# An expert layer in two forms: 96 tokens gather the rows of their picked experts, 160 stay dense in plain float32

## The reference

```python
# 8 heads, 128 x 128 = 16384 single-neuron experts, top 16 per head: 128 picks a token
s1 = einsum('thd,kd->thk', q[:, :, 0], sub_k1);  v1, i1 = top_k(s1, 16)
s2 = einsum('thd,kd->thk', q[:, :, 1], sub_k2);  v2, i2 = top_k(s2, 16)
cand = (v1[..., :, None] + v2[..., None, :]).reshape(T, 8, 256)
vals, ci = top_k(cand, 16)
idx = i1[ci // 16] * 128 + i2[ci % 16];  gates = softmax(vals)
# for a token t with its 128 picks k:
h = einsum('tkd,td->tk', expert_u[idx], x)
a = gelu(h) * gates
out = einsum('tk,tkd->td', a, expert_v[idx])
```

## Time and profile before

| | us |
|---|---|
| median of 3 runs (1588.82 to 1589.45) | 1589.16 |
| span of the profiled execution | 1587.9 |
| the expert layer in it, 249.8 to 1023.7 | 773.9 |
| TensorE busy | 1556.2 |
| VectorE busy | 1253.3 |
| ScalarE busy | 806.6 |
| GpSimd busy | 105.1 |

### The profile page before, as it was taken

One profiled execution on the slowest core, in us unless ns is written; L12 is line 12 of the kernel. 1 busy time (PEld: TensorE's weight loads), 2 busy tenths in 40 slices (PEclk: granted clock), 3 DMA queues, 4 the chain that ended last, 5 costly groups with the idle time before them and its releaser, 6 DMA issues.

```text
span 1587.9 us, 26239 instructions
## 1 busy us (share of the span) xinstructions
PE 1556.2 (98%) x9128; PEld 1364.8 (86%) x9128; DVE 1253.3 (79%) x2167; ACT 806.6 (51%) x1231; POOL 105.1 (7%) x67
## 2 busy tenths in 40 slices
PE   8999899999999999999999999999999999999998
PEld 7888799999999888888888888888887988778886
DVE  5575669989999777777777777887878988688777
ACT  5545545457776333444444444554445757554444
POOL 0000177700000000000000000000000000000000
PEclk9999999999999999999999999999999999999999
DMA  5544444533334555555555555555554433445552
GB/s 219 192 153 176 158 149 168 180 142 110 106 109 182 190 202 189 187 183 186 188 193 193 192 185 185 198 197 187 190 185 147 162 130 107 159 166 192 185 185 106
DMA packets 39389, 270.47 MB, mean 170 GB/s; under 512 B 4881, under 2 KB 5393, under 8 KB 7074
## 3 DMA queue, kind: packets, MB, share of 16 engines
q1 hardware_dynamic: 37440, 266.45, 47.3%
q10 hardware_dynamic: 1890, 3.24, 0.6%
HBM read 268.62 MB, written 1.05 MB: 170 GB/s over the span
## 4 chain that ended last, share of the span: by engine, by line
PE 80%; DVE 14%; issue 3%; ACT 2%; DVEq 1%; DMA 0%; SPq 0%; ACTq 0%
PE ps L737 52%; PE ps L770 17%; PE ps L772 7%; DVE wlo L567 2%; DVE wlo L2171 2%; DVE raw L2142 2%; PE ps L769 1%; DVE XT L1899 1%; DVE wlo L2142 1%; DVE whi L2142 1%; DVE arena L2519 0%; PE ps L1013 0%; PE ps L1202 0%; PE ps L980 0%; DVE raw L2155 0%
## 5 line engine op out<-in xcount | busy, mean ns | idle before, releaser
L770 PE MATMUL ps<-XT,whi 128*128 128x512 f32 x1200 | 429.2, 398 | 2.9 <-DVE XT L1899 1.9
L737 PE MATMUL ps<-XT,whi 128*128 128x256 f32 x1696 | 311.0, 285 | 1.6 <-DVE wlo L567 0.9
L772 PE MATMUL ps<-XT,wlo 128*128 128x256 f32 x1050 | 294.5, 281 | 0.0
L550 ACT ACTIVATE whi<-raw 128x1024 fp32r<-128x1024 f32 x194 | 204.3, 1059 | 171.8 <-PE ps L737 130.5
L737 PE MATMUL ps<-whi,HAh 128*128 128x512 f32 x696 | 272.2, 391 | 1.0 <-DVE wlo L567 0.8
L737 PE MATMUL ps<-wlo,HAh 128*128 128x512 f32 x696 | 271.2, 390 | 0.0
L737 PE MATMUL ps<-whi,HAl 128*128 128x512 f32 x696 | 270.8, 389 | 0.0
L567 DVE TENSOR_TENSOR wlo<-raw,whi 128x1024 fp32r<-128x1024 f32 x174 | 211.1, 1221 | 71.3 <-ACT whi L550 69.6
L737 PEld LDWEIGHTS ps<-XT,whi 128*128 128x128 f32 x1696 | 263.6, 192 | 2.3 <-DVE wlo L567 1.3
L770 PEld LDWEIGHTS ps<-XT,whi 128*128 128x128 f32 x1200 | 222.4, 188 | 49.4 <-issue 2.3
L737 PE MATMUL ps<-XT,wlo 128*128 128x256 f32 x848 | 239.8, 283 | 0.0
(11 more groups left out here) (292 smaller groups left out, 1919.9 us busy)
## 6 DMA issues: line engine op xcount, KB each, us to landing
raw<-in_experts SPq DMA_DIRECT2D x128, 1024.0 KB, 4.7
raw<-in_panels SPq DMA_DIRECT2D x58, 1024.0 KB, 4.8
raw<-in_ffa SPq DMA_DIRECT2D x33, 1024.0 KB, 4.8
raw<-in_ffb SPq DMA_DIRECT2D x33, 1024.0 KB, 4.7
arena<-in_row_post ACTq DMA_DIRECT2D x3, 512.0 KB, 4.5
X<-in_x SPq DMA_DIRECT2D x2, 512.0 KB, 5.6
arena<-in_row_ln ACTq DMA_DIRECT2D x2, 256.0 KB, 4.1
arena<-in_row_post SPq DMA_DIRECT2D x1, 512.0 KB, 5.7
```

The costliest lines, as they stand in the source:

```text
L550: act.activation(whi[:, buf(p), :], half(item_of(p), p % 2), ACT.Copy).then_inc(part_hi, 1)
L737: last = pe.matmul(out, x if w_moving else w, w if w_moving else x, start=start and n == 0, stop=stop and n == 2)
L770: last = pe.matmul(out, wh[:, k], XT[:, k], start=k == 0, stop=k == NK - 1)
L772: pe.matmul(out[:, T:], wl[:, k], XTh[:, k], start=False, stop=False)
```

## The change

The 256 tokens are divided. Tokens 0 to 95 (SPARSE, on partitions 0 to 95 of tile 0) take only the rows that they picked: for pick k, GpSimd issues an indirect DMA that fetches row ROWS[t, k] of `peer_u` for each of the 96 tokens into one of six buffers (the six parts of whi and wlo). VectorE multiplies it with the token's normed row XROW and sums (`dots_to`), ScalarE makes the GELU in four lots of 32, VectorE multiplies with the softmax weights (AS), GpSimd fetches the rows of `peer_v`, and VectorE adds each, scaled, to X or XACC in turn (`row_sum`). The sequence is 128 gathers of u, then 128 of v; gather n waits until the buffer of n - 6 is used.

Tokens 96 to 255 (TD = 160) stay dense. TensorE reads the raw items as they are, in plain float32, against XF (160 columns, float32) and G (128 x 160). No part of this layer is split, so ScalarE's and VectorE's (and GpSimd's) weight parts are gone. All hidden passes come first: FIRST = 56 early, BESIDE = 60 beside 20 groups of gates (three a group), LATE = 12 behind them; then all 128 output passes, with the expert rows as the stationary operand and G as the moving one, so that the result stands with features on partitions in three banks, is copied to OT by ScalarE, transposed by TensorE ("ext") and added to X by VectorE. The top 16 are taken for tile 0 first, then come its picks and ROWS, and then tile 1; two dots stand in each group on VectorE. The loops written with Fori are unrolled. SyncE loads a slot again when TensorE has used its item (h_done, a_used).

```diff
+SPARSE = 96
+TD = T - SPARSE
+GROUPS = TD // ONES
+FIRST = 56
+BESIDE = 3 * GROUPS
+LATE = P - FIRST - BESIDE
+BUFS = 6
@@ GpSimd
+            pool.wait_ge(rows_ready, 1)
+            for n in range(2 * P):
+                if n == P:
+                    pool.wait_ge(sel_ready, 1)
+                    pool.memset(OT[:, :, 0:SPARSE], 0.0).then_inc(pad_zero, 1)
+                if n >= BUFS:
+                    pool.wait_ge(row_used, n - BUFS + 1)
+                pool.indirect_dma_start(
+                    out=GATHERED[n % BUFS], out_offset=None, in_=(peer_u, peer_v)[n // P][:, :],
+                    in_offset=bass.IndirectOffsetOnAxis(ap=ROWS[0:SPARSE, n % P:n % P + 1], axis=0))\
+                    .then_inc(row_here[n % BUFS], 16)
@@ TensorE
+            def hidden(n, out):
+                w = expert_in(n).rearrange("p (k e) -> p k e", k=NK)
+                for k in range(NK):
+                    last = pe.matmul(out[:, 0:TD], w[:, k], XF[:, k, :], start=k == 0, stop=k == NK - 1)
+                last.then_inc(h_done, 1)
+            for g in range(GROUPS):
+                for n in range(3 * g, 3 * g + 3):
+                    if n >= 2:
+                        pe.wait_ge(beside_done, n - 1)
+                    hidden(FIRST + n, ps[:, n % 2])
                 pe.wait_ge(one_ready, g + 1)
                 pe.wait_ge(one_scaled, g + 1)
+                if g >= 2:
+                    pe.wait_ge(gate_out, g - 1)
+                    pe.wait_ge(gate_mul, g - 1)
+                gate_products(g % 2)
+            for n in range(BESIDE, BESIDE + LATE):
+                pe.wait_ge(beside_done, n - 1)
+                hidden(FIRST + n, ps[:, n % 2])
...
+            for c in range(P):
...
+                w = expert_in(P + c)
+                for s in range(NK):
+                    at = s % PER_BANK
+                    last = pe.matmul(bank(EX[s // PER_BANK])[:, TD * at:TD * at + TD], w[:, P * s:P * s + P], G[:, c, :],
+                                     start=c == 0 and at == 0, stop=c == P - 1, skip_group_check=True)
@@ ScalarE
+            act.dma_start(XROW, row_post[4:5, :].broadcast_to([P, D])).then_inc(row_in, 16)
+            for k in range(NK):
...
+                last = act.activation(XF[:, k, :], t_bank("n2", k // 2)[:, T * (k % 2) + SPARSE:T * (k % 2) + T], ACT.Copy,
+                                      scale=col("norm2", k))
+            last.then_inc(xf_ready, 1)
@@ VectorE
+            def dots_to(n):
+                for k in range(dots[0], n):
+                    u = gathered(k)
+                    dve.tensor_tensor_reduce(u, u, XROW[0:SPARSE], 1.0, 0.0, ALU.mult, ALU.add, HS[0:SPARSE, k:k + 1])\
+                       .then_inc(row_used, 1)
...
+            def row_sum(k):
+                v = gathered(P + k)
+                a, into = AS[0:SPARSE, k:k + 1], (X[0:SPARSE, 0, :], XACC[0:SPARSE])[k % 2]
...
+                    ins = dve.scalar_tensor_tensor(into, v, a, into, ALU.mult, ALU.add)
+                ins.then_inc(row_used, 1)
...
+            for i in range(PEER_H // 2):
+                top_heads(i, 0)
+            picks(0)
+            dve.scalar_tensor_tensor(ROWS[0:SPARSE], ...).then_inc(rows_ready, 1)
+            for i in range(PEER_H // 2):
+                top_heads(i, 1)
+                dots_to(4 * i + 4)
...
+            one_hots(0, 0)
+            for g in range(GROUPS):
+                if g + 1 < GROUPS:
+                    one_hots(g + 1, (g + 1) % 2)
                 if g:
+                    dve.wait_ge(gate_mul, g)
+                for n in range(3 * g, 3 * g + 3):
+                    beside_times(n)
+                dots_to(20 + 2 * g + 2)
+                dve.wait_ge(beside_done, 3 * g + 3)
+                gate_times(g, g % 2)
+            for n in range(BESIDE, BESIDE + LATE):
+                dve.wait_ge(gate_out, GROUPS)
+                beside_times(n)
+                dots_to(20 + 2 * GROUPS + 2 * (n - BESIDE))
+            for i in range(4):
+                dots_to(max(dots[0], 32 * i + 32))
+                dve.wait_ge(row_gelu, i + 1)
...
+            for k in range(P):
+                row_sum(k)
+            dve.wait_ge(row_used, 2 * P)
+            link(dve.tensor_tensor(X[0:SPARSE, 0, :], X[0:SPARSE, 0, :], XACC[0:SPARSE], ALU.add))
```

More of the change, by code:

```diff
@@ L142 @@
 assert _parts == S_EXP
[L143 to L152, removed]
+EX = [f"ex{i}" for i in range(-(-NK // PER_BANK))]
+_use(*[(n, "act") for n in EX])
 def _feed_forward(base, last):
@@ L608, in stream @@
                     load(item0 + j, src[j])
[L610 to L619, removed]
+            for j in range(P):
+                load(EXP0 + j, experts[j])
             sp.dma_start(FG, row_post[0:1, :].broadcast_to([P, D])).then_inc(final_in, 16)
@@ L1040, in _ @@
-            exps = [bank(f"ex{i}") for i in range(4)]
-            def expert(n, u, b):
-                pe.wait_ge(part_lo, n * 2 + (S_EXP + 3))
-                pe.wait_ge(h_sum, n + (1 - EARLY))
-                hidden_wide(u, b)
-                output(n, u + 1, n * 2 + (S_EXP + 4), b)
-            def output(n, p, lo, b, start=False, stop=False):
-                pe.wait_ge(part_lo, lo)
-                pe.wait_ge(a_ready, n + 1)
-                last = v_part(exps, p, hidden_acts(b), start, stop, BY_HALF)
-                if stop:
-                    for ins in last:
-                        ins.then_inc(main_done, 1)
-                else:
-                    last[-1].then_inc(a_used, 1)
@@ L1087, in feed_forward @@
+            pe.wait_ge(pad_zero, 1)
+            read_out(pe, EX[-1])
+            transposes("ext", [OT[:, 4 * hf + q, P * tt:P * tt + P] for hf in range(2) for tt in range(DENSE0, NT)
+                               for q in range(4)])
             def feed_forward(s0, base, outs):
@@ L1297, in limit @@
             def limit(p):
-                for end in (S_PRE, S_END):
+                for end in (S_EXP, S_END):
                     if p < end:
@@ L2069, in top16 @@
                 link(ins)
[L2071 to L2079 removed]
+            dve.wait_ge(row_in, 16)
@@ L2176, in _ @@
-            parts[0] = S_PRE
-            split_to(S_PRE)
-            for n in range(2):
-                tile = slice(0, P)
-                link(dve.tensor_copy(HAh[:, n, tile], G[:, n, tile]))
-                dve.tensor_tensor(HAl[:, n, tile], G[:, n, tile], HAh[:, n, tile].bitcast(f32), ALU.subtract)\
-                   .then_inc(first_tile, 1)
-            split_to(S_PRE + 1)
-            dve.wait_ge(beside_done, BESIDE - 1)
-            gate_times(BESIDE - 1, 1)
-            beside_times(BESIDE - 1, 1, BESIDE - 1)
@@ L2652 @@
     v = a["peer_v"][0].reshape(P, P, D).transpose(1, 0, 2)
[L2653 to L2654 removed]
+    experts = items(np.concatenate([u, v]))
     def ffn(n):
```

529 lines of the change are left out of this document (204 added, 325 removed).

## The result

The kernel became slower: 1687.69 us (median of 4 runs, 1682.6 to 1693.25) against 1589.31 us of the kernel before (1588.82 to 1591.29), a ratio of 1.061 with a 95% interval of 1.059 to 1.064. The forecast was 1521 us, and the range given, 1490 to 1660, does not hold the time. The profiled execution has a span of 1680.9 us.

A forecast was written before the change was run, and what follows sets the result against it. TensorE was taken to bound the kernel, with the DMA bounding the new output passes. Stages end at 251.8, 372, 574, 608, 951, next stage 956 against 1023.7: 1589.2 - 68 = 1521 us, range 1490 to 1660.

The forecast's parts named there:

- First 56 experts: Early hidden passes: 56 x 2.14 = 120 us on TensorE, to 372, with VectorE's picks and 20 dots ready at 369.
- 20 groups: Gates with three hidden passes each: first turn adds 12 us, then 19 turns of 10.0, together 202 us, to 574.
- The ring of waits: In each group, gate_times, one-hots, beside_times, hidden pass, GELU, two dots and handovers wait on each other: 10.0 us a turn.
- Last 12 hidden passes: Behind the groups, each waits for VectorE's 0.31 + 2 x 1.25 = 2.85 us: 34 us, to 608.
- Output passes to the last row sum: DMA bounds the output stage: 133.2 MB of experts and gathers at 388 GB/s, 343 us, to 951; TensorE needs 273.
- rival 3: VectorE's dots cost two passes, 2.3 us, +1.1 each: 1611 us; chance 0.07.
- Rival 1: Gathered rows crowd on half the DMA's paths, 1.25 us a gather, output stage 371 us: 1549 us; chance 0.18.
- The rule on the partitions: Skill's rule for DMA into SBUF: partitions 0 to 63 reach only half of the 16 ports; gathers fill 96 partitions.
- Rival 2: GpSimd's gather issue bounds last hidden and output passes; slower from 2.32 us a gather, 1720 us at 3; chance 0.25.
- The sign of this rival: In the output passes, GpSimd issuing gathers back to back with the DMA share under 0.8.
- under 2 us: GpSimd's issue of one gather takes less than this, so it hides under the DMA's 2.04 us per gather.
- Rival 4: Group waits overlap better, at TensorE's 8.1 us (-38), with DMA at 418 GB/s (-24): 1459 to 1483 us; chance 0.06.

The follow-up runs named there:

- e7: The change with its 96 gathering tokens spread three in every four over all partitions, every fourth row skipped by the gather: 1550.73 us, 0.974 of the kernel before.
- e1: The change with each gather replaced by a one-column memset on GpSimd, no rows moved, VectorE working on stale buffers: 1435.3 us.
- e8: The kernel with 96 tokens spread three in every four, with 34 dots ahead of the groups instead of 20: 1528.79 us, 0.962 of the kernel before.
- e2: The change with each gather replaced by GpSimd's plain load of 96 consecutive rows, not the picked ones, into the same buffers: 1684.46 us.
- e6: The change with 128 gathering tokens instead of 96 and 68 first experts instead of 56, the whole layer computed: 1555.62 us, 0.977 of the kernel before.
- e5: The change with every gather fetching 128 rows to partitions 0 to 127, of which VectorE uses 96: 1576.83 us.
- e4: The change with gathers fetching only rows 0 to 63 of the list, to partitions 32 to 95; the other 32 tokens' rows left out: 1462.72 us.

## Why the prediction was wrong

The chain ended on the stage that was named, the output passes, and by the engine that was named, the DMA. The step that failed is the term of the sum in it: "133.2 MB take 319 to 375 us. I take 388 GB/s, the middle, since the dense items run like the rows of both ends". The experts' items do not run so beside the gathers: with both, the full DMA moved 292 GB/s, with the gathers almost alone 264, and the stage took 488 us instead of 343. The cause that the runs show is the place of the rows: with 96 rows on partitions 0 to 95 both kinds of packets took longer, and with 96 rows spread over all partitions (e7) the rate was 411.

Step by step, forecast against the trace (last ends for the layer's parts, in us):

- Start of the layer 251.8; it came at 253.3 (+1.5).
- First 56 experts to 372; TensorE took the next work, the transposes, at 395.1. The stage is 22 us longer than forecast. The chain from 252 to 392 has 38.5% in landings of experts' items: the first gathers already starved TensorE, in a stage for which the forecast counted no transfer at all (from 300 to 392 share 0.93, 289 GB/s). TensorE's matmuls waited 10.8 us for items, and after such rests part of the work ran at the lower clock: the granted clock was 0.95 over the stage, and the same work kept TensorE busy for 130 us. Without gathers (e1) the clock was 1.00 and the next work began at 372.9, as forecast. VectorE, which the forecast had ready at 369, was ready at 390, because ScalarE's exponential stands behind the GELU of expert 52: VectorE waited 32.3 us for it. I had not counted that wait; it was late with TensorE, so it cost the groups nothing, and e8 uses the room.
- 20 groups, 202 us at 10.0 a turn: 187 us (395 to 582) at 9.24. Two turns of the change, at line 1018:

```profile
506.45 1.95 PE L1018 MATMUL ps<-xt_plain 128*128 128x128 f32 x16
...
515.69 1.95 PE L1018 MATMUL ps<-xt_plain 128*128 128x128 f32 x16
```

  The ring of waits over VectorE's line was right, and 0.8 us a turn too long.
- Last 12 hidden passes 34 us: 41, to 622.9. Here VectorE's dots wait for rows (58% of the chain from 582 to 623 is the landing of gathered rows).
- Output passes to the last row sum, 343 us: 488, from 622.9 to 1111.0. That is +145 of the 167 us by which the time was missed; the steps of the layer make 157 together, 4 lie behind the layer, and the rest is that the profiled execution was quicker than the median of the runs.
- Behind it +5: TensorE's transposes start 2.1 us later, at 1113.1.
- Plain float32, 2.14 us for an expert, and 273 us for 128: e1 shows 278 where nothing hinders TensorE. The dot (1220 ns, and 79 for reading its sum) and the row sum (1280 ns) cost what was taken, so rival 3 falls.

Rival 1 had the right place, the crowded partitions, and I gave it 0.18. It had the wrong size: 1549 us where 1688 was measured. It priced a gather at 4/3 of 0.94, 1.25 us, where 1.44 was measured, and it left the experts' items at their full rate, 2.51 us each. Its 4/3 was near right for the gather itself (1.44 against e7's 1.11 is 1.30); what it lacked is that the experts' packets slow down as well, by 1.42. Together the output stage had to move 133.2 MB, and at the 292 and 264 GB/s measured that is 456 to 505 us, not the 371 of the rival. Its "against", that 96 divides by 16, counted rows per engine and not rows per path. The rule on the partitions was beside it with the very partitions; I treated it as a small correction, since no row of the trace before shows a transfer of 96 partitions. From the figure of the Trainium skill, "SBUF — State Buffer", section "Door 1: The DMA port swizzle (why [64,N] ≈ [32,N])", of 435 GB/s over 16 ports, an estimate for 8 rows of 4 KB on one port is 1.20 us a gather; 1.44 was measured, and 1.47 from one to the next where the gathers run alone.

Rival 2 was wrong for the change as it stands: GpSimd's issue took 1.05 to 1.40 us in the mean with 0.30 beside it, below the 2.32 from which the kernel would be slower by it. The suspicion behind it has something: where GpSimd issues while VectorE waits for rows (660 to 790), an issue takes 0.91 us, and in the groups, where VectorE works, mostly 1.66 or 2.74 us, 1.84 in the mean; the plain loads of e2 keep 505 ns there. The groups had room for it. The sign of this rival shows only when the rows run well: 1.79 us a gather in e7's tail, where the skip of rows may be part of it. The forecast's "under 2 us" is right in the mean, but "hides under the DMA's 2.04 us" fails for the tail, where only gathers are left and a gather's transfer needs 1.11.

Rival 4 did not come either: the groups ran at 9.24 us and not at 8.1.

With the rows spread evenly, e7 moves 411 GB/s, more than the 388 that the forecast assumed, and still its output stage takes 381 us and not 343, because of the tail; it ends 30 us above the forecast. e8, which takes 14 dots more ahead of the groups, ends 8 us above, in part by luck: its rate is higher than the forecast's and its tail has no term in it.

What stays open: by which mechanism the crowded rows slow the experts' items, whose own packets lie evenly. The gathers need no neighbour to be slow (266 GB/s alone from 1000 to 1100), and the experts' items land in 4.8 us in the median without gathers (e1), but no run shows what the two share. And whether the skip makes the issue dearer: its mean for the second table is 1.36 us in e7, 1.16 to 1.25 in e8 and 1.05 to 1.08 in e6, but the skip was not tried by itself.

## What to carry to other kernels

Price a transfer by where its rows land, and not by its bytes alone: with 64 or 96 rows from partition 0 on this kernel took 1630 and 1688 us, with 128 rows 1577, because each row took longer and what ran beside it paid as well. Use all 128 partitions, or spread the rows so that both halves get the same. Where a full DMA is the forecast, the rate has to come from a row with the same partitions; if none is there, the crowded cost belongs in the sum, for all transfers of the stage. And when a transfer is made cheap, look at what remains when its neighbour ends: here the issue of the gathers.

## What the runs showed that I had not expected

- A third more bytes made the kernel 111 us faster (e5: 134.23 MB in 354 us of the 16 engines; the change: 100.68 MB in 368 us).
- Crowded rows slow the neighbours: the experts' queue, the same 266.45 MB, took 797 us beside 96 crowded rows and 817 beside 64, but 705 to 723 beside rows that lie evenly (e4 to e8). Without any gathers it took 740 (e1) and 751 (before), so differences of some 40 us mean little here, and 80 to 110 do.
- Late items cost TensorE more than the waits here. In the first 56 experts of the change it waited 10.8 us for items and was busy 130 us at a mean granted clock of 0.95; the same work kept it busy 120 us in e1, at 1.00.
- A gather with skipped rows counts their packets (36864 in e7, as many as with 128 rows) at 100.71 MB, and its issue took 1.32 us on GpSimd in the median of the second table, against 0.95 in e6; a plain load of 96 rows issued by GpSimd took 0.505 us.
